# Order of the recurrence's scale levels and the projection matmuls between them

## The chip, the cores and the metric
The kernel runs on one core of a Trainium2 chip. The time is that of the device, in microseconds, of one execution of the whole program; a kernel's time is the median of its runs. Before the change it is 2439.49 us (three runs, 2434.9 to 2441.67).

## What is computed
An encoder trunk of one layer is applied to two requests, x_sample (1024 tokens) and x_prompt (512 tokens), with shared weights. The part that matters here is the recurrence of the mixer, for each of four heads and in both directions:

```python
q = silu(hq);  v = hi
f_f = lb[0] + (1 - lb[0]) * sigmoid(hff);  f_b = lb[1] + (1 - lb[1]) * sigmoid(hfb)
# per chunk, forward direction; the backward one is the same on flipped inputs
S_new = exp(b_last)[..., None] * S + einsum('bhsk,bhsv->bhkv', kc * exp(b_last - b), vc)
A = einsum('bhtk,bhsk,bhtsk->bhts', qc, kc, dec)        # dec: products of gates between s and t
o = einsum('bhts,bhsv->bhtv', A, vc) + einsum('bhtk,bhkv->bhtv', qc * exp(b), S)
hgo = rms_norm(o_f + o_b) * silu(hg)
```

Before it stands one input projection (h @ w_in), from which hq, hff, hfb, hi and hg come; around it stand an attention, an output projection and an expert layer with 16 experts.

## The kernel before
`build` runs, for the sample group and then the prompt group, `normalise`, `hgrn`, `attention` and `project_out`; then the experts and a last norm. The recurrence is `hgrn` (L543).

Tiling. Tokens lie along the free dimension, in blocks of 512 (`BLK`), `NB` = 2 blocks for the sample group and 1 for the prompt group. A block has four chunks of 128 (`BC`). Score banks `X[0..3]` are PSUM banks, one for each chunk of a block.

Levels. Instead of the three-index product of the reference, the scores of a chunk are made at eight scale levels. At level k TensorE multiplies the keys and queries as they stand, in small tiles on the diagonal (L688 for k < 6, 32x32 tiles; L694 for k = 6; L699 for k = 7), for the forward direction (d = 0, tiles q_f and k_f) and the backward one (d = 1, q_b and k_b). VectorE then multiplies gates into q and k for the next level (L819 for k = 0, L826, L827 and L829 for others), and this may begin when the level's products have been made (`level_read`); TensorE's next level waits for it (`updated`). After level 7 the step `diag` has VectorE multiply each score bank by masks (L870) and sum it up (L875); the next block's level 0 overwrites the banks and so waits for L870 (`masked`). Then keys are transposed (`k_rows`, L710, copied by ScalarE L796), states are made (`state`, L719, and VectorE L888 and L891), then the output (`o`, L739), its norm (`squares`, `mean`, `norm`: L804, L899, L952, L904) and its transpose (`mix`, L747, L912).

The projection for the next head is done beside it, by `Projection` (L410 and on). There are five columns (V, Q, FF, FB, G), each in two halves: ten units. A unit is the product of four 128x128 weight tiles with each block of tokens, as three matmuls each (high and low parts: L472, L473, L474), so 12 matmuls for each block. Its weights are split into `w_hi` (ScalarE, L453, waits until the unit before the last has been summed) and `w_lo` (VectorE, L457, waits for `w_hi`); TensorE's first matmul of a unit waits for `w_lo`. `w_hi` and `w_lo` have two slots; `w_raw`, loaded by SyncE (L447), has five, and a load waits for the split that frees its slot. When a column's two units are done it is landed by ScalarE (L767), the columns Q and G by VectorE too (L844).

Order. Each engine works through one list of steps, in order. `slots` is the list of recurrence steps; `beside` (L490) puts pieces of the projection between them: `piece(n)` is half a unit for one block (`CUTS` = 2: two weight tiles, 6 matmuls), and ahead of a unit's first piece it puts the step ("split", u + 1) for ScalarE and VectorE, behind a column's last piece ("land", column). `run_heads` runs three lists: the projection alone, a loop over three heads with both, and the last head's recurrence alone. Before the change the pieces are shared out evenly, one for each step (squares and mean not counted), with NB more at the start. Attention uses another function, `beside_at`, whose pieces are whole units for one block.

Of the kernel before, what the change touches and what calls it, by code (L numbers as in the profile page):

```python
# [15 lines left out]
P = 128  # L16
D = 1024
DT = D // P
BLK = 512
BC = BLK // P  # L20
# [4 lines left out]

COL_AQ, COL_AK, COL_AV, COL_HQ, COL_HFF, COL_HFB, COL_HI, COL_HG = range(0, 8 * BLK, BLK)
HALF = DT // 2
CUTS = 2
EXPERTS = 16
FF = 1024  # L30
FT = FF // P
# [455 lines left out]
        return steps  # L487


def beside(slots, proj, lead=0):  # L490


    pieces = CUTS * proj.units * proj.NB
    out, done, passed = [("split", 0)], 0, 0
    counted = lambda step: step[0] not in ("squares", "mean")
    total = sum(map(counted, slots))
    for step in slots:
        out.append(step)
        passed += counted(step)
        upto = lead + (pieces - lead) * passed // total  # L500
        for n in range(done, upto):
            out += proj.piece(n)
        done = upto
    return out


# [36 lines left out]
def hgrn(nc, g, T, w_in, masks_in, consts, banks, mem, chosen):  # L543
# [5 lines left out]
    NT, NB = T // P, T // BLK  # L549
    ident, slope_cols, lb, one_minus_lb, neg_lam, att_g, hg_g, carried, minus_half = consts  # L550
    with ExitStack() as c:
        sem = c.enter_context(semaphores(nc, f"h{g}"))
        X, FAR, TURN = banks[0:4], banks[4], banks[5]
        V, Q, FF_, FB, G = range(5)
        proj = Projection(sem, T, [COL_HI, COL_HQ, COL_HFF, COL_HFB, COL_HG], 5, [Q, G], banks[6:8], w_in, mem)
# [3 lines left out]
        level_read = [Signal(sem(f"level_{d}"), 8 * NB) for d in "fb"]  # L559
# [5 lines left out]
        v_rows = Signal(sem("v_rows"), NB)  # L565
        far_placed = Signal(sem("far_placed"), NB)
# [3 lines left out]
        gates = Signal(sem("gates"), 2)  # L570
        updated = [Signal(sem(f"updated_{d}"), 8 * NB) for d in "fb"]
# [14 lines left out]
        ds_bank = lambda d, b: (2 * d + b + 1) % 4  # L586
        slots = [("start",)] + [("v_rows", b) for b in range(NB)]
        for b in range(NB):
            slots += [("level", b, k) for k in range(8)] + [("diag", b)]
        for d in range(2):  # L590
            slots += [("k_rows", d, b) for b in range(NB)]
            slots += [("state", d, b) for b in (range(NB) if d == 0 else reversed(range(NB)))]
# [4 lines left out]
        first = beside([("none",)], proj)  # L597
        if g == 1:
            first = with_choices(first, "split", range(CHOICES_BEFORE["attention"][0]))
        stages = first, beside(slots, proj, NB), slots  # L600
        in_order = [s for s in slots if s[0] == "state"]
        nth = lambda step: in_order.index(step)
        first_state = lambda b, n, d: (b * BC + n == 0) if d == 0 else (b * BC + n == NT - 1)
# [1 line left out]
        x_uses = []  # L605
        for s in range(4):
            uses = []
            for step in slots:
                if step[0] == "level" and step[2] == 0:
                    uses.append((step, masked, BC * step[1] + s))  # L610
                if step[0] == "k_rows" and kt_bank(*step[1:]) == s:
                    uses.append((step, k_rows, NB * step[1] + step[2]))
                if step[0] == "state" and ds_bank(*step[1:]) == s:
                    d, b = step[1:]
                    done = min((b + 1) * BC, NT - 1) if d == 0 else min((NB - b) * BC, NT - 1)
                    uses.append((step, state[d], done - 1))
            x_uses.append(Uses(uses))
        far_uses = Uses([(("level", b, 6), far_placed, b) for b in range(NB)]
                        + [(("o", b), normed, b) for b in range(NB)])
        if NB == 2:  # L620
            far_uses = Uses([(("level", b, 6), far_placed, b) for b in range(NB)] + [(("o", 0), normed, 0)])
            x_uses[0].uses.append((("o", 1), normed, 1))
        o_bank = lambda b: FAR if b == 0 else X[0]
        o_uses = lambda b: far_uses if b == 0 else x_uses[0]
# [16 lines left out]
        with nc.Block() as block:  # L641
# [14 lines left out]
            def _(pe):  # L656
                start_signals(pe, [proj.summed, v_turned, *level_read, k_turned, added, o_summed, o_turned])

                def body(step, i, j):
# [3 lines left out]
                    elif kind == "v_rows":  # L663
                        b = step[1]
                        pe.wait_ge(proj.land_act.sem, proj.land_act.at(i, NB * V + b))
                        pe.wait_ge(*turn_uses.before(i, step))
                        for n in range(BC):
                            at = b * BLK + n * P
                            mm = pe.transpose(TURN[:, n * P:(n + 1) * P], mem.land[V][:, at:at + P], ident[:])
                        mm.then_inc(v_turned.sem, 1)  # L670
                    elif kind == "level":
                        b, k = step[1:]
                        if k == 6:
                            pe.wait_ge(*far_uses.before(i, step))
                        for d in range(2):
                            if k == 0:
                                pe.wait_ge(q_taken.sem, q_taken.at(i, d))
                                pe.wait_ge(k_made.sem, k_made.at(i, d))
                            else:
                                pe.wait_ge(updated[d].sem, updated[d].at(i, 8 * b + k - 1))  # L680
                            q, kk = mem.q[d], mem.k[d]
                            for n in range(BC):
                                at = b * BLK + n * P
                                if k == 0 and d == 0:
                                    pe.wait_ge(*x_uses[n].before(i, step))
                                if k < 6:
                                    for z in range(0, P, 32):
                                        mm = pe.matmul(X[n][z:z + 32, (6 * d + k) * 32:(6 * d + k + 1) * 32],  # L688
                                                       kk[:, at + z:at + z + 32], q[:, at + z:at + z + 32],
                                                       start=True, stop=True, tile_position=(0, z))  # L690
                                elif k == 6:
                                    for z in range(0, P, 64):
                                        s, t = z + 32 * d, z + 32 * (1 - d)
                                        mm = pe.matmul(FAR[s:s + 32, n * 96:n * 96 + 32], kk[:, at + s:at + s + 32],  # L694
                                                       q[:, at + t:at + t + 32], start=True, stop=True,
                                                       tile_position=(0, s))
                                else:
                                    s, t = 64 * d, 64 * (1 - d)
                                    mm = pe.matmul(FAR[s:s + 64, n * 96 + 32:n * 96 + 96], kk[:, at + s:at + s + 64],  # L699
                                                   q[:, at + t:at + t + 64], start=True, stop=True,  # L700
                                                   tile_position=(0, s))
                            mm.then_inc(level_read[d].sem, 1)
                    elif kind == "k_rows":
                        d, b = step[1:]
                        bank, uses = X[kt_bank(d, b)], x_uses[kt_bank(d, b)]
# [2 lines left out]
                        for n in range(BC):  # L708
                            at = b * BLK + n * P
                            mm = pe.transpose(bank[:, n * P:(n + 1) * P], mem.k[d][:, at:at + P], ident[:])  # L710
                        mm.then_inc(k_turned.sem, 1)
                    elif kind == "state":
                        d, b = step[1:]
# [8 lines left out]
                    elif kind == "o":  # L722
                        b = step[1]
# [7 lines left out]
                        for n in range(BC):  # L731
# [79 lines left out]
            def _(dve):  # L811
# [3 lines left out]
                def level(d, b, k, i):  # L815

                    if k == 0:
                        q = mem.q[d][:, b * BLK:(b + 1) * BLK]
                        dve.tensor_tensor(q, q, products(d, b, 0), ALU.mult).then_inc(updated[d].sem, 1)  # L819
                        return  # L820
                    half = 1 << (k - 1)
                    n = BLK // (2 * half)
                    q, kk = halves(mem.q[d], b, half), halves(mem.k[d], b, half)
                    f = products(d, b, k - 1).rearrange("p (n a) -> p n a", a=2)
                    late, early = (1, 0) if d == 0 else (0, 1)
                    dve.tensor_tensor(products(d, b, k), f[:, :, 0], f[:, :, 1], ALU.mult)  # L826
                    dve.tensor_tensor(q[:, :, late, :], q[:, :, late, :],  # L827
                                      f[:, :, early:early + 1].to_broadcast([P, n, half]), ALU.mult)
                    dve.tensor_tensor(kk[:, :, early, :], kk[:, :, early, :],  # L829
                                      f[:, :, late:late + 1].to_broadcast([P, n, half]),  # L830
                                      ALU.mult).then_inc(updated[d].sem, 1)

                def body(step, i, j):
# [19 lines left out]
                                              lb[:, bass.ds(i + d * HEADS, 1)], ALU.mult,  # L853
                                              ALU.add).then_inc(gates.sem, 1)
                    elif kind == "level":
                        b, k = step[1:]
                        for d in range(2):

                            dve.wait_ge(level_read[d].sem, level_read[d].at(i, 8 * b + k))
                            if k == 0:  # L860
                                dve.wait_ge(gates.sem, gates.at(i, d))
                            else:
                                dve.wait_ge(updated[d].sem, updated[d].at(i, 8 * b + k - 1))
                            level(d, b, k, i)
                    elif kind == "diag":
                        b = step[1]
                        for n in range(BC):
# [1102 lines left out]
```

## Time and profile before

| | us |
|---|---|
| median of the runs | 2439.49 (2434.9 to 2441.67) |
| span of the profiled execution, first to last instruction | 2427.6 |
| TensorE matmul busy | 2095.0 (86% of the span) |
| weight loads busy | 1801.6 (74%) |
| VectorE busy | 1484.0 (61%) |
| ScalarE busy | 1116.1 (46%) |
| GpSimd busy | 228.3 (9%) |
| mean granted clock of TensorE | 0.930 of full speed |
| loop of `hgrn`, sample group: starts of its passes and its end | 108.1, 197.5, 288.8, 378.8 |
| the same, prompt group | 986.9, 1032.4, 1077.8, 1124.3 |

The profiled execution's own time outside the span isn't given by the profile; the median of the runs lies 11.9 us above the span. The starts of passes are those of ScalarE's copy of the queries (L773).

How to read it. A timeline row has the start (us), the duration (us) of the group, the engine (PE is TensorE's matmul, PEld its weight load, DVE VectorE, ACT ScalarE, POOL GpSimd), the line, the operation, the tiles out<-in, their sizes, the count, and in brackets the idle time of the engine before it with what ended it. A window row has the stretch, its length, then the busy time of PE, PEld, DVE, ACT and POOL (with counts), the granted clock of TensorE as a part of full speed, the DMA share and GB/s. Matmuls overlap one another: their pace is the distance of two starts, not their duration. A level's products appear as two records each.

### The profile page before, as it was taken

Reading aid. Unit: us, or ns where it says so; the run is one execution under the profiler, and the core shown is the slowest. Engines: PE = TensorE matmul, PEld = TensorE weight load, DVE = VectorE, ACT = ScalarE, POOL = GpSimd, SP = SyncE. Lnnn points to the kernel's source line nnn. Section 1 sums busy time; section 2 is a strip of 40 time slices with the busy share of each in tenths; the row PEclk is TensorE's granted clock in tenths of the full one; section 3 lists DMA queues with packets and bytes.
Section 4 is the critical chain, followed back from the end, with each engine's and each line's share of the span. In section 5 each row is a group of like instructions: output and inputs, shape, how many; then the busy total and the mean of one; then the engine's idle time right before and its main releaser. Section 6 shows DMA issues by size and latency. Waiting matters only on the chain. (4 is left out here: it accounts for less than half of the span.)

```text
span 2427.6 us, 44323 instructions
## 1 busy us (share of the span) xinstructions
PE 2095.0 (86%) x16110; PEld 1801.6 (74%) x16110; DVE 1484.0 (61%) x2662; ACT 1116.1 (46%) x1941; POOL 228.3 (9%) x364
## 2 busy tenths in 40 slices
PE   4999997799897795998785849999999999999990
PEld 3777775577775684776574749999999999999990
DVE  3275577256666333667567756676666676666662
ACT  3222221256565323232464236666666666666652
POOL 1001101000000000111000001111111111111101
PEclk9999996899999896998897869999999999999995
DMA  3111100100000433220212257787777777777756
GB/s 116 45 30 33 32 11 2 56 22 19 22 4 1 151 119 107 67 57 9 77 43 85 98 184 225 241 250 235 252 241 242 241 245 237 238 243 244 237 169 229
DMA packets 178341, 313.16 MB, mean 129 GB/s; under 512 B 11825, under 2 KB 78001, under 8 KB 178225
## 3 DMA queue, kind: packets, MB, share of 16 engines
q1 hardware_dynamic: 169328, 280.08, 34.8%
q0 software_dynamic: 7168, 25.17, 5.2%
q10 hardware_dynamic: 1728, 6.29, 0.6%
q8 instruction: 82, 1.34, 0.2%
q14 instruction: 35, 0.28, 0.0%
HBM read 280.04 MB, written 31.46 MB: 128 GB/s over the span
## 5 line engine op out<-in xcount | busy, mean ns | idle before, releaser
L1802 DVE TENSOR_TENSOR we_lo<-raw,we_hi 128x1024 fp32r<-128x1024 f32 x384 | 466.0, 1223 | 219.4 <-ACT we_hi L1750 219.4
L1716 PE MATMUL psum<-x_parts,we_hi 128*128 128x384 f32 x2048 | 585.4, 360 | 2.9 <-DVE we_lo L1802 2.9
L1718 PE MATMUL psum<-x_parts,we_lo 128*128 128x192 f32 x2048 | 513.5, 251 | 0.0
L1750 ACT CAST we_hi<-raw 128x1024 fp32r<-128x1024 f32 x384 | 399.3, 1052 | 185.3 <-PE psum L1718 100.7
L1718 PEld LDWEIGHTS psum<-x_parts,we_lo 128*128 128x128 f32 x2048 | 392.3, 192 | 0.6
L1716 PEld LDWEIGHTS psum<-x_parts,we_hi 128*128 128x128 f32 x2048 | 385.5, 188 | 3.6 <-issue 3.0
L472 PE MATMUL psum<-hT_hi,w_hi 128*128 128x512 f32 x768 | 325.7, 424 | 62.1 <-DVE w_lo L457 62.0
L473 PE MATMUL psum<-hT_lo,w_hi 128*128 128x512 f32 x768 | 308.1, 401 | 0.0
L474 PE MATMUL psum<-hT_hi,w_lo 128*128 128x512 f32 x768 | 308.1, 401 | 0.0
L472 PEld LDWEIGHTS psum<-hT_hi,w_hi 128*128 128x128 f32 x768 | 149.2, 194 | 101.4 <-DVE w_lo L457 44.8
L474 PEld LDWEIGHTS psum<-hT_hi,w_lo 128*128 128x128 f32 x768 | 149.1, 194 | 33.7
L473 PEld LDWEIGHTS psum<-hT_lo,w_hi 128*128 128x128 f32 x768 | 149.9, 195 | 26.6
L457 DVE TENSOR_TENSOR w_lo<-h_w_raw,w_hi 128x512 fp32r<-128x512 f32 x80 | 57.3, 716 | 90.8 <-ACT w_hi L453 90.8
L767 ACT ACTIVATE h_land<-psum 128x512 f32<-128x512 f32 x60 | 35.9, 598 | 157.5 <-PE psum L474 157.4
L453 ACT CAST w_hi<-h_w_raw 128x512 fp32r<-128x512 f32 x80 | 49.3, 617 | 127.4 <-PE psum L474 115.5
L1732 PE MATMUL psum<-we_hi,hid_parts 128*128 128x512 f32 x256 | 103.0, 402 | 0.0
L1736 PE MATMUL psum<-we_lo,hid_parts 128*128 128x512 f32 x256 | 100.9, 394 | 0.0
L1735 PE MATMUL psum<-we_hi,hid_parts 128*128 128x512 f32 x256 | 100.8, 394 | 0.0
L1734 PE MATMUL psum<-we_hi,hid_parts 128*128 128x512 f32 x256 | 100.8, 394 | 0.0
L1733 PE MATMUL psum<-we_lo,hid_parts 128*128 128x512 f32 x256 | 100.6, 393 | 0.0
L121 POOL TENSOR_TENSOR carried_pool<-minus_half 128x1 f32<-128x1 f32 x48 | 13.7, 285 | 844.9 <-ACT result_s L1790 692.0
L1112 PEld LDWEIGHTS psum<-v_rows,k_rows 128*128 128x128 f32 x640 | 80.1, 197 | 16.9 <-ACT k_rows L1170 14.4
(245 smaller groups left out, 3598.4 us busy)
## 6 DMA issues: line engine op xcount, KB each, us to landing
raw<-in_w_gate SPq DMA_DIRECT2D x128, 512.0 KB, 4.6
raw<-in_w_up SPq DMA_DIRECT2D x128, 512.0 KB, 6.2
raw<-in_w_down SPq DMA_DIRECT2D x128, 512.0 KB, 5.7
h_w_raw<-in_w_in SPq DMA_DIRECT2D x80, 256.0 KB, 2.8
a_w_raw<-in_w_in SPq DMA_DIRECT2D x48, 256.0 KB, 2.8
o_land<-in_w_out SPq DMA_DIRECT2D x16, 512.0 KB, 5.2
y<-y_rows SPq DMA_DIRECT2D x12, 512.0 KB, 6.4
h_land<-in_x_s SPq DMA_DIRECT2D x8, 512.0 KB, 4.2
```

The source lines that it names most:

```text
L472: pe.matmul(out[:], mem.w_hi[:, u % 2, n, :], hi, start=(k == 0), stop=False)
L473: pe.matmul(out[:], mem.w_hi[:, u % 2, n, :], lo, start=False, stop=False)
L474: mm = pe.matmul(out[:], mem.w_lo[:, u % 2, n, :], hi, start=False, stop=(k == DT - 1))
L1716: pe.matmul(out[:, 0:2 * SLOTS], w_hi[:, s, at], x_parts[:, k, :, :], start=(k == 0), stop=False, skip_group_check=True)
L1718: mm = pe.matmul(out[:, SLOTS:2 * SLOTS], w_lo[:, s, at], x_hi[:, k, :], start=False, stop=(k == DT - 1), skip_group_check=True)
L1732: pe.matmul(out[2 + h][:], a, u, start=first, stop=False)
L1733: pe.matmul(out[2 + h][:], a, v, start=False, stop=False)
L1734: pe.matmul(out[2 + h][:], b, u, start=False, stop=last)
L1735: pe.matmul(out[h][:], both, u, start=first, stop=False)
L1736: mm = pe.matmul(out[h][:], both, v, start=False, stop=last)
L1750: act.copy(w_hi[:, n % PARTS, :], raw[:, s, :]).then_inc(hi.sem, 1)
L1802: dve.tensor_tensor(w_lo[:, n % PARTS, :], raw[:, n % RAW, :], w_hi[:, n % PARTS, :].bitcast(F32), ALU.subtract).then_inc(lo.sem, 1)
```

## The change
`CUTS` becomes 4: a piece is one weight tile for one block, 3 matmuls. The step ("level", b, k), which did both directions, becomes two steps ("level", b, k, d), on TensorE and VectorE. `beside` takes fixed numbers of pieces behind steps of some kinds: 2 behind `start`, 2 behind each `v_rows`, 1 behind each level of a direction, 6 behind each `diag`; the rest is shared evenly over the other steps. Waits belong to the same operations as before.

```diff
-CUTS = 2
+CUTS = 4
...
-def beside(slots, proj, lead=0):
+def beside(slots, proj, fixed=None):
...
+    fixed = {"squares": 0, "mean": 0} | (fixed or {})
     pieces = CUTS * proj.units * proj.NB
-    out, done, passed = [("split", 0)], 0, 0
-    counted = lambda step: step[0] not in ("squares", "mean")
-    total = sum(map(counted, slots))
+    rest = pieces - sum(fixed.get(step[0], 0) for step in slots)
+    others = sum(step[0] not in fixed for step in slots)
+    out, done, shared, passed = [("split", 0)], 0, 0, 0
     for step in slots:
         out.append(step)
-        passed += counted(step)
-        upto = lead + (pieces - lead) * passed // total
-        for n in range(done, upto):
+        if step[0] in fixed:
+            now = fixed[step[0]]
+        else:
+            passed += 1
+            now = rest * passed // others - shared
+            shared += now
+        for n in range(done, done + now):
             out += proj.piece(n)
-        done = upto
+        done += now
     return out
...
-            slots += [("level", b, k) for k in range(8)] + [("diag", b)]
+            slots += [("level", b, k, d) for k in range(8) for d in range(2)] + [("diag", b)]
...
-        stages = first, beside(slots, proj, NB), slots
+        stages = first, beside(slots, proj, {"start": 2, "v_rows": 2, "level": 1, "diag": 6}), slots
...
                     elif kind == "level":
-                        b, k = step[1:]
-                        if k == 6:
+                        b, k, d = step[1:]
+                        if k == 6 and d == 0:
                             pe.wait_ge(*far_uses.before(i, step))
-                        for d in range(2):
...
                     elif kind == "level":
-                        b, k = step[1:]
-                        for d in range(2):
-
-                            dve.wait_ge(level_read[d].sem, level_read[d].at(i, 8 * b + k))
...
+                        b, k, d = step[1:]
+                        dve.wait_ge(level_read[d].sem, level_read[d].at(i, 8 * b + k))
```

The lists of the prompt group's loop from level 5 to the first key transposes, written out (mmN is N matmuls; the sample group's are of the same kind, with 24 matmuls to a unit):

```
before  [level 5] split5 mm6 [level 6] mm6 [level 7] split6 mm6 [diag] mm6 land-FF [k_rows f] split7 mm6
after   [level 5 f] mm3 [level 5 b] mm3 land-Q [level 6 f] split5 mm3 [level 6 b] mm3 [level 7 f] mm3
        [level 7 b] mm3 [diag] split6 mm12 land-FF split7 mm6 [k_rows f] mm6
```

In the sample group, block 0: before, `[level 7] split4 mm6 [diag] mm12 [level 0 of block 1]`; after, `[level 7 b] mm3 [diag] mm6 split4 mm12 [level 0 f of block 1]`. The pieces between a pass's start and its first level go from 30 matmuls to 18 (sample) and from 18 to 12 (prompt).

## Rows read from the trace of the kernel before

**Rows 1.** The page: its first line, with the span.
```profile
span 2427.6 us, 44323 instructions
```

**Rows 2.** Windows: eight levels of the sample group's first pass.
```profile
118.80:135.60 16.80, 16.80 (x475) 12.70 (x474) 12.98 (x42) 2.32 (x4) 0.00 (x0) 1.00 0.12 35
```

**Rows 3.** Timeline of TensorE: a piece of six, a level, and the next piece.
```profile
119.61 0.50 PE L472 MATMUL psum<-hT_hi,w_hi 128*128 128x512 f32 x1
...
121.20 0.35 PEld L688 LDWEIGHTS psum<-q_f,k_f 128*32 128x32 f32 x32 [0.36 <-issue]
121.20 0.46 PE L688 MATMUL psum<-q_f,k_f 128*32 128x32 f32 x32
...
121.48 0.49 PE L688 MATMUL psum<-q_b,k_b 128*32 128x32 f32 x32
...
121.90 0.50 PE L472 MATMUL psum<-hT_hi,w_hi 128*128 128x512 f32 x1
...
122.23 0.39 PE L473 MATMUL psum<-hT_lo,w_hi 128*128 128x512 f32 x1
122.24 0.19 PEld L474 LDWEIGHTS psum<-hT_hi,w_lo 128*128 128x128 f32 x1
...
122.46 0.39 PE L474 MATMUL psum<-hT_hi,w_lo 128*128 128x512 f32 x1
```

**Rows 4.** Timeline and windows: the second pass, behind the mask sum of block 0.
```profile
232.81 0.79 PE L472 MATMUL psum<-hT_hi,w_hi 128*128 128x512 f32 x1
...
236.55 0.49 PE L472 MATMUL psum<-hT_hi,w_hi 128*128 128x512 f32 x1
...
229.40:240.00 10.60, 8.36 (x209) 5.87 (x209) 9.03 (x19) 1.11 (x2) 2.35 (x8) 0.84 0.08 22
```

**Rows 5.** Timeline of TensorE: first level products and key transposes of passes; 142.27 between.
```profile
118.77 0.32 PE L688 MATMUL psum<-q_f,k_f 128*32 128x32 f32 x14
...
142.27 0.27 PE L688 MATMUL psum<-q_f,k_f 128*32 128x32 f32 x8 [1.03 <-DVE h_masked L870]
...
162.68 0.38 PE L710 MATMUL psum<-ident,k_f 128*128 128x128 f32 x2
...
208.09 0.30 PE L688 MATMUL psum<-q_f,k_f 128*32 128x32 f32 x12
...
253.94 0.27 PE L710 MATMUL psum<-ident,k_f 128*128 128x128 f32 x1
...
299.36 0.24 PE L688 MATMUL psum<-q_f,k_f 128*32 128x32 f32 x4
...
344.48 0.38 PE L710 MATMUL psum<-ident,k_f 128*128 128x128 f32 x2
...
992.77 0.32 PE L688 MATMUL psum<-q_f,k_f 128*32 128x32 f32 x14
...
1013.09 0.38 PE L710 MATMUL psum<-ident,k_f 128*128 128x128 f32 x2
```

**Rows 6.** Timeline: the prompt group's level 7 and mask sum, on TensorE and VectorE.
```profile
1009.33 0.27 PE L699 MATMUL psum<-q_f,k_f 128*64 128x64 f32 x1
...
1010.04 0.16 DVE L826 TENSOR_TENSOR h_fend_f<-h_fup_f 128x4 f32<-128x4 f32 x1 [0.63 <-PE psum L699]
...
1010.79 0.16 DVE L826 TENSOR_TENSOR h_fend_b<-h_fup_b 128x4 f32<-128x4 f32 x1
...
1012.14 0.55 DVE L870 TENSOR_TENSOR h_masked<-psum,h_masks 128x384 f32<-128x384 f32 x1
...
1017.64 0.68 DVE L457 TENSOR_TENSOR w_lo<-h_w_raw,w_hi 128x512 fp32r<-128x512 f32 x1
...
1018.37 0.50 PE L472 MATMUL psum<-hT_hi,w_hi 128*128 128x512 f32 x1 [0.58 <-DVE w_lo L457]
```

**Rows 7.** Windows: the starts of two passes.
```profile
105.00:113.50 8.50, 6.41 (x22) 4.84 (x21) 4.94 (x6) 3.60 (x6) 3.58 (x6) 0.80 0.11 32
1029.00:1036.00 7.00, 4.91 (x22) 3.71 (x21) 3.26 (x6) 2.66 (x5) 2.18 (x4) 1.00 0.13 37
```

More of the change, by code:

```diff
@@ L608, in hgrn @@
             for step in slots:
-                if step[0] == "level" and step[2] == 0:
+                if step[0] == "level" and step[2:] == (0, 0):
                     uses.append((step, masked, BC * step[1] + s))
@@ L617, in hgrn @@
             x_uses.append(Uses(uses))
-        far_uses = Uses([(("level", b, 6), far_placed, b) for b in range(NB)]
+        far_uses = Uses([(("level", b, 6, 0), far_placed, b) for b in range(NB)]
                         + [(("o", b), normed, b) for b in range(NB)])
         if NB == 2:
-            far_uses = Uses([(("level", b, 6), far_placed, b) for b in range(NB)] + [(("o", 0), normed, 0)])
+            far_uses = Uses([(("level", b, 6, 0), far_placed, b) for b in range(NB)] + [(("o", 0), normed, 0)])
             x_uses[0].uses.append((("o", 1), normed, 1))
@@ L671, in body @@
                     elif kind == "level":
-                        b, k = step[1:]
-                        if k == 6:
+                        b, k, d = step[1:]
+                        if k == 6 and d == 0:
                             pe.wait_ge(*far_uses.before(i, step))
-                        for d in range(2):
-                            if k == 0:
-                                pe.wait_ge(q_taken.sem, q_taken.at(i, d))
-                                pe.wait_ge(k_made.sem, k_made.at(i, d))
-                            else:
[L680 to L702, printed above, removed]
@@ new lines, in body @@
+                        if k == 0:
+                            pe.wait_ge(q_taken.sem, q_taken.at(i, d))
+                            pe.wait_ge(k_made.sem, k_made.at(i, d))
+                        else:
+                            pe.wait_ge(updated[d].sem, updated[d].at(i, 8 * b + k - 1))
+                        q, kk = mem.q[d], mem.k[d]
+                        for n in range(BC):
+                            at = b * BLK + n * P
+                            if k == 0 and d == 0:
+                                pe.wait_ge(*x_uses[n].before(i, step))
+                            if k < 6:
+                                for z in range(0, P, 32):
+                                    mm = pe.matmul(X[n][z:z + 32, (6 * d + k) * 32:(6 * d + k + 1) * 32],
+                                                   kk[:, at + z:at + z + 32], q[:, at + z:at + z + 32],
+                                                   start=True, stop=True, tile_position=(0, z))
+                            elif k == 6:
+                                for z in range(0, P, 64):
+                                    s, t = z + 32 * d, z + 32 * (1 - d)
+                                    mm = pe.matmul(FAR[s:s + 32, n * 96:n * 96 + 32], kk[:, at + s:at + s + 32],
+                                                   q[:, at + t:at + t + 32], start=True, stop=True,
+                                                   tile_position=(0, s))
+                            else:
+                                s, t = 64 * d, 64 * (1 - d)
+                                mm = pe.matmul(FAR[s:s + 64, n * 96 + 32:n * 96 + 96], kk[:, at + s:at + s + 64],
+                                               q[:, at + t:at + t + 64], start=True, stop=True,
+                                               tile_position=(0, s))
@@ L703, in body @@
+                        mm.then_inc(level_read[d].sem, 1)
                     elif kind == "k_rows":
@@ L855, in body @@
                     elif kind == "level":
-                        b, k = step[1:]
-                        for d in range(2):
-                            dve.wait_ge(level_read[d].sem, level_read[d].at(i, 8 * b + k))
[L860 to L864, printed above, removed]
+                        b, k, d = step[1:]
+                        dve.wait_ge(level_read[d].sem, level_read[d].at(i, 8 * b + k))
+                        if k == 0:
+                            dve.wait_ge(gates.sem, gates.at(i, d))
+                        else:
+                            dve.wait_ge(updated[d].sem, updated[d].at(i, 8 * b + k - 1))
+                        level(d, b, k, i)
                     elif kind == "diag":
```

## The prediction, made before the changed kernel was timed
> **What bounds the kernel now.** I read the page first: the span is 2427.6 us [rows 1], and the diff touches only the loop over heads of `hgrn`. So I looked up where that loop lies: three passes for the sample group (1024 tokens, 108 to 379 us) and three for the prompt group (512 tokens, 987 to 1124 us), some 408 us together. The pass after each loop ("alone") has the same order before and after, the pass ahead of it has no levels, and attention takes its matmuls through another function, in the same order whether cut in two or four. Everything else of the span stays.
>
> Within a pass I read the table of windows. Over eight levels of the sample group TensorE is busy for all 16.80 us and VectorE for 12.98 of them [rows 2]. The few places of a pass where TensorE does wait are counted below. Elsewhere TensorE's own work sets the pace, and a level's products are not what anything waits for. The reader should then ask two things of the change: does it add work to TensorE, and does it take away or make waits of TensorE.
>
> **What a change of shape costs (the price of a cut).** In [rows 3] the six-matmul piece begins at 119.61 and the level's first product at 121.20, 1.59 us later. The steady pitch of these matmuls is 0.23 (122.23 to 122.46), six are 1.38. The other 0.21 are the two edges: 0.33 instead of 0.23 behind the first matmul (121.90 to 122.23), and as much ahead of the level. The forward direction then takes 0.28 (121.20 to 121.48), and the backward one, with the piece's first matmul behind it, 0.42 (121.48 to 121.90). One level is 0.70 + 1.59 = 2.29 us.
> In the changed order each direction stands alone: 0.42, and a piece of three: 3 x 0.23 + 0.21 = 0.90. Two of each are 2.64. A level costs 0.35 more. Levels inside the loop: 16 in each of three sample passes, 8 in each of three prompt passes, 72 together: 72 x 0.35 = +25.2 us. The trace of before has no direction alone between pieces. From below, the piece's two edges alone are 0.21, 15 us in all; from above, the idle time of 0.36 of the weight load ahead of a level [rows 3] and the 0.14, 36 us in all. I take 0.35, since each of its parts is a gap between starts in the same rows. A gain I exclude: no matmul goes away, and nothing in [rows 2] is left for it to fill.
>
> In [rows 3] the weight load of a level (128x32) waits 0.36 with the ending named as issue, while the load of a wide matmul starts at 122.24, with the matmul of 122.23 still under way. The Trainium skill, page "TensorE: Matmul & The Clock Gate", section "Architectural detail: the array is 16× 32×32, not 1× 128×128", says that TensorE's queue is a partial reorder window which can pull weight loads ahead of matmuls in flight. By that rule the cut would cost nothing, which is rival B. The wide loads agree with it, the level's loads do not.
>
> **Waits of the sample passes.** From a pass's first level product to its first key transpose the trace has 162.68 - 118.77 = 43.91, 253.94 - 208.09 = 45.85 and 344.48 - 299.36 = 45.12 us [rows 5]. Without a wait I get 16 levels x 0.70 (an estimate for the last two levels, which have other shapes) + 14 pieces x 1.59 + the 18 matmuls around the first mask sum, 4.35 + the last 12, 2.87 = 40.7. So the waits are 3.2 + 5.1 + 4.4 = 12.8 us. The largest stands at the mask sum of block 0: TensorE's next level needs the four score banks, and gets them as VectorE masks them, the last at 142.27 [rows 5]. Twice the clock falls behind it: the level from 232.81 to 236.55 takes 3.74 instead of 2.29, with a granted clock of 0.84 in the stretch around it [rows 4], so half speed (1.2 GHz) for part of it.
> Now 21 matmuls stand between the last product of level 7 and the next level, where 18 stood, and the weight split that VectorE did ahead of the masks now stands behind them. Counted from the start of that last product: TensorE is through after 0.5 + 0.1 + 21 x 0.23 + 0.1 = 5.5 us. VectorE starts the level's update after 0.71, takes 0.75, and its fourth mask ends 3 x 1.38 + 0.55 later, at 6.15 [rows 6] (the same operations in the prompt group). About 0.6 of the wait stays, and 0.2 where the query tile lands between two levels. I take 0.8 a pass: 12.8 - 2.4 = -10.4 us. Bounds: 0 and -12.8. Block 1's mask sum has no such wait before or after: key transposes follow it, and the split of unit 6 is ahead of it.
>
> **The split behind the prompt group's mask sum.** Here a unit has only 12 matmuls. At the mask sum the new list has: mask sum, split 6, the four pieces of unit 5, land, split 7, two pieces of unit 6, key transposes. VectorE works its list in order, so `w_lo` of unit 6 is made only when the whole mask sum is done; TensorE's first matmul of unit 6 waits for it, and the transposes, states and output of the head are queued behind that matmul. Before, split 6 stood ahead of the mask sum. Counted from the start of the last product of level 7: VectorE 0.71 (1009.33 to 1010.04) + 0.75 (to 1010.79) + mask sum 5.50 (1012.14 to 1017.64) + split 0.68 + 0.05 = 7.7 [rows 6]. TensorE 0.5 + the level's three matmuls and twelve of unit 5, 3.5 = 4.0. It stands still for 3.7 us, in three passes: +11.1. Bounds: 3.0 to 4.5 each, as VectorE is level with TensorE or late from level 6.
> A wait like that lets the clock fall: at the starts of passes, where TensorE waits about 2.2 us for the first split, it fell in four of six ([rows 7] has one of each kind, 0.80 and 1.00). One fall costs 3.74 - 2.29 = 1.45 us [rows 4]; 3 x 1.45 = +4.4, bound below by nothing.
> What goes in the prompt passes: of 1013.09 - 992.77 = 20.32 us [rows 5] 19.6 is work by the same count, 0.7 waits, and TensorE's 0.58 for the split at 1018.37 [rows 6], which was late behind the mask sum and now follows at once on split 6. Together 1.3 x 3 = -3.9.
>
> **Edits with no price.** At the start of a pass 12 fewer matmuls (6 in the prompt group) stand ahead of level 0; they come back later in the same in-order list, so TensorE's total is the same. Keys and gates are ready by then (GpSimd's and ScalarE's parts begin when the pass begins). The last piece of a pass is 9 or 6 matmuls instead of 12 behind the last transpose: VectorE's mix is over before the landing either way. ScalarE's splits move with VectorE's, and wait for nothing new. SyncE's load of a weight slot waits for the split that frees it; a slot is used again five units later, 60 matmuls of 0.23 us in the prompt group, so that split 6 comes some 4 us later is hidden; should it not be, ScalarE's next splits would be late by as much.
>
> **The sum.** 25.2 - 10.4 + 11.1 + 4.4 - 3.9 = +26.4 us. On the profiled span of 2427.6 that is 2454.0. Around the span lie 11.9 us up to the median of 2439.49; I count them as unchanged: 2465.9 us. The likeliest case's own spread is about 2456 to 2476. A measurement of this kernel can tell about 0.3%, 7 us, from no change.
>
> **Rivals.**
> A. The late split is absorbed: VectorE reaches the prompt group's mask sum earlier than I count, and nothing of the 15.5 us for wait and clock comes. 2450.4 us, still slower. Against it: VectorE cannot start the mask sum before the last update, and 5.5 us stand against 3.5. Chance 0.07.
> B. Cuts are free: level loads are pulled ahead when only three matmuls stand before them. Without the 25.2 us: 2440.7, no difference. Against it, the 0.33 us starts in [rows 3] came with operands ready. Chance 0.07.
> C. VectorE's chain (levels, masks, states, norm) sets a pass's length, and TensorE's matmuls only fill. Then the cuts fit in, and what counts is that level 0 starts 12 (6) matmuls earlier: 3 x (2.8 + 1.4) = 12.6 us, 2426.9, faster. It decides as soon as TensorE has over 0.35 us idle in a level; [rows 2] shows none. Chance 0.04.
> D. The clock falls within the levels too, as wide matmuls are a smaller part of each (1.38 of 2.64 instead of 2.29). With two falls a pass, 12 x 1.45 = 17.4 more: 2483.3. For it, falls at [rows 4]; against it, those came behind a wait. Chance 0.06.
> My sum has 0.76.
> The range 2449 to 2478 takes in my case and A. Slower by over 0.3%: 0.76 + 0.07 + 0.06 less a little for a sum that comes out small, 0.87; within 0.3%: 0.08; faster: 0.05.
>
> **What would show it.** In the windows, a sample pass longer by about 2 us and a prompt pass by about 7. In TensorE's timeline, a level of 2.6 us with its two directions apart and 0.33 at four edges; if the edges were at 0.23 the first term is wrong. At the prompt group's mask sum, the first matmul of unit 6 released by `w_lo`, 3.7 us late, and a granted clock of half behind it. At the sample group's block 0, the wait for the masks down from 2.1 to about 0.6 us. The prediction is wrong if the levels' pace is not TensorE's, or if the late split waits for something else.

## The result

| | median us (runs) | ratio to before, 95% interval |
|---|---|---|
| before | 2439.53 (4; 2434.9 to 2441.67) | |
| changed | 2463.33 (4; 2459.17 to 2464.37) | 1.0101 (1.0085 to 1.0117) |

The change costs 23.8 us, 1%; the forecast was +26.4, to 2465.9. Page of the changed kernel, its first line and its busy times, with their share of the span and the number of instructions; [rows 1] is the first line of before:

```profile
span 2457.0 us, 44323 instructions
PE 2119.0 (86%) x16110; PEld 1802.5 (73%) x16110; DVE 1488.4 (61%) x2662; ACT 1117.4 (45%) x1941; POOL 229.8 (9%) x364
```

No instruction was added, and TensorE's matmul busy time grew from 2095.0 to 2119.0. The profiled execution took 2459.17, 2.2 us more than its span. If the same lies around the span of before (2427.6), that profiled execution took about 2430, 10 us less than its kernel's median. So the two profiles differ by 29.4 us and the medians by 23.8. I therefore compare kernels in two ways: by their medians, and by the length of the passes in the profile. Windows over the three sample passes, then over the three prompt passes, first of before, then of the changed kernel (stretch, length, busy times of PE, PEld, DVE, ACT, POOL, granted clock, DMA):

```profile
108.14:378.77 270.63, 257.61 (x3640) 204.42 (x3640) 167.17 (x420) 66.96 (x169) 32.73 (x72) 0.97 0.09 26
986.95:1124.26 137.31, 127.78 (x1816) 100.06 (x1816) 90.58 (x225) 41.34 (x102) 19.31 (x45) 0.99 0.17 48
```
```profile
106.53:382.54 276.01, 267.61 (x3640) 200.76 (x3640) 170.26 (x420) 67.50 (x169) 34.93 (x72) 0.99 0.09 26
991.18:1152.88 161.70, 144.52 (x1816) 106.84 (x1816) 91.66 (x225) 42.19 (x103) 19.34 (x45) 0.92 0.14 41
```

The reader sees 5.4 us more in the sample group and 24.4 more in the prompt group, together 29.8; outside the passes nothing moved by more than 1.6 us. VectorE's own time in the passes grew by 4.2 us. The granted clock went up a little in the sample passes and down to 0.92 in the prompt passes. Since the low level is half of full speed, a mean of 0.92 means that a steadily busy TensorE falls behind by 8% of the time: 161.7 x 0.08 = 13 us, against 137.3 x 0.01 = 1.4 before.

The levels, in TensorE's timeline of the changed kernel; [rows 3] has the same place before:

```profile
114.15 0.46 PE L692 MATMUL psum<-q_b,k_b 128*32 128x32 f32 x32
114.54 0.50 PE L472 MATMUL psum<-hT_hi,w_hi 128*128 128x512 f32 x1
114.88 0.39 PE L473 MATMUL psum<-hT_lo,w_hi 128*128 128x512 f32 x1
...
115.43 0.46 PE L692 MATMUL psum<-q_f,k_f 128*32 128x32 f32 x32
115.82 0.50 PE L472 MATMUL psum<-hT_hi,w_hi 128*128 128x512 f32 x1
...
116.72 0.46 PE L692 MATMUL psum<-q_b,k_b 128*32 128x32 f32 x32
```

A direction with its piece of three takes 1.28 us (114.15 to 115.43), the two of a level 2.57 (114.15 to 116.72), where a level of before took 2.29. The edges are as they were, 0.34 behind the first wide matmul (114.54 to 114.88) and 0.32 ahead of the next level (115.11, the start of the last wide matmul, to 115.43). Six levels of the first prompt pass show the same over a longer stretch; the row of 1006.63 is of before, whose level 0 starts at 992.77 [rows 5], the other two are of the changed kernel:

```profile
1006.63 0.35 PE L694 MATMUL psum<-q_f,k_f 128*32 128x32 f32 x10
```
```profile
995.65 0.45 PE L692 MATMUL psum<-q_f,k_f 128*32 128x32 f32 x30
...
1011.06 0.44 PE L698 MATMUL psum<-q_f,k_f 128*32 128x32 f32 x15
```

From level 0 to level 6 before took 13.86 us, 2.31 a level, and the changed kernel 15.41, 2.57 a level. The single level of [rows 3], 2.29, was a little short of the mean.

The prompt group's late split, on both engines ([rows 6] has the place before):

```profile
1015.11 0.68 PE L703 MATMUL psum<-q_b,k_b 128*64 128x64 f32 x8
...
1016.57 0.55 DVE L872 TENSOR_TENSOR h_masked<-psum,h_masks 128x384 f32<-128x384 f32 x1
...
1021.29 0.80 DVE L877 TENSOR_REDUCE h_diag<-h_masked 128x32 f32<-128x384 f32 x1
1022.00 1.28 DVE L457 TENSOR_TENSOR w_lo<-h_w_raw,w_hi 128x512 fp32r<-128x512 f32 x2
...
1022.82 0.79 PE L472 MATMUL psum<-hT_hi,w_hi 128*128 128x512 f32 x1 [3.40 <-DVE w_lo L457]
1023.40 0.63 PE L473 MATMUL psum<-hT_lo,w_hi 128*128 128x512 f32 x1
```

The mask sum ends, the splits of units 6 and 7 follow, and TensorE starts unit 6 after 3.40 us without work. Then its second matmul comes 0.58 behind the first, where at full clock it is 0.33. The window behind the wait:

```profile
1022.20:1029.00 6.80, 6.18 (x17) 4.93 (x18) 1.08 (x2) 0.59 (x1) 2.36 (x8) 0.50 0.27 77
```

The clock is at its lower level, 1.2 GHz, for 6.8 us, twice as long as I had counted.

What TensorE's matmuls waited for, in the list of waits over the sample passes (total us, times, longest), first before, then the changed kernel:

```profile
PE psum L472 <- DVE w_lo L457: 6.3, 3, 2.1
PE psum L688 <- DVE h_masked L870: 5.1, 6, 1.0
PE psum L688 <- issue: 1.9, 3, 0.8
PE psum L688 <- DVE k_b L829: 0.5, 1, 0.5
```
```profile
PE psum L472 <- DVE w_lo L457: 6.3, 3, 2.1
PE psum L472 <- DVE h_land L848: 1.8, 3, 0.6
PE psum L692 <- DVE h_masked L872: 0.8, 3, 0.3
```

The wait for the masks did fall from 5.1 to 0.8 us, the others of the levels from 2.4 to nothing, and one of 0.6 in each pass is new. With two small rows not shown (0.5 us, L743) the sum is 9.4 us, against 13.8 before. The first row is the wait at the start of a pass; it is 6.3 us in every kernel below too.

### The profile page after: what moved, and what is told of

It is laid out like the page before. It is cut to its first block and busy times, and to the rows that moved or that the text cites. A ratio compares the mean times of both kernels' runs of the same rounds, so it can differ in the third digit from the quotient of the medians.

```text
span 2457.0 us, 44323 instructions
## 1 busy us (share of the span) xinstructions
PE 2119.0 (86%) x16110; PEld 1802.5 (73%) x16110; DVE 1488.4 (61%) x2662; ACT 1117.4 (45%) x1941; POOL 229.8 (9%) x364
## 5 line engine op out<-in xcount | busy, mean ns | idle before, releaser
L472 PE MATMUL psum<-hT_hi,w_hi 128*128 128x512 f32 x768 | 335.7, 437 | 72.7 <-DVE w_lo L457 70.8
L1381 PE MATMUL psum<-hT_hi,w_hi 128*128 128x512 f32 x192 | 78.8, 410 | 15.5 <-DVE hT_lo L1499 15.5
```

What stands on the lines that cost most here:

```text
L472: pe.matmul(out[:], mem.w_hi[:, u % 2, n, :], hi, start=(k == 0), stop=False)
```

## The experiments

In the tables "passes" are the sample and prompt passes of each profile, by length, with the granted clock over them.

### The split back ahead of the mask sum (e1)

```diff
-        stages = first, beside(slots, proj, {"start": 2, "v_rows": 2, "level": 1, "diag": 6}), slots
+        both = beside(slots, proj, {"start": 2, "v_rows": 2, "level": 1, "diag": 6})
+        if NB == 1:
+            at = both.index(("diag", 0))
+            both.remove(("split", 6))
+            both.insert(at, ("split", 6))
+        stages = first, both, slots
```

> The changed kernel with one step moved: in the prompt group's loop the split of unit 6 stands ahead of the mask sum again, on ScalarE and VectorE. My theory: the wait of TensorE for that split (3.4 us, three times) and the low clock behind it go, 15.5 us by the terms of the sum; the mask sum now begins behind the split, so the next split (unit 7) may come up to 0.9 us late in each pass: 2448 to 2451 us. Rival A (the late split is absorbed, the cuts are all of the loss): 2463, as the changed kernel.

Measured: 2445.93 us (12 runs), ratio 1.003 (1.0017 to 1.0043); 17.4 us less than the changed kernel. Its passes:

```profile
107.41:381.83 274.42, 266.05 (x3640) 199.58 (x3640) 170.17 (x420) 67.45 (x168) 34.86 (x72) 0.99 0.09 26
994.81:1138.31 143.50, 134.30 (x1816) 99.61 (x1816) 91.94 (x225) 41.86 (x102) 19.25 (x45) 0.99 0.16 46
```

The prompt passes account for it (161.70 to 143.50, 18.2 us; the sample passes differ by 1.6), and their clock is back at 0.99. One step of 0.7 us on VectorE, moved past a step of 5.5 (ScalarE's half of the split moves with it), is worth 0.7% of the kernel. The spans of the two profiles differ by 7.8 us only (2457.0 and 2449.2): the stretch outside the passes, which no edit here touches, took 2019.3 us in the one and 2031.3 in the other, and lies between 2019.3 and 2031.6 in the profiles whose passes are given here. So medians and passes are compared, not spans. The next split is late now, as the expectation had it:

```profile
1027.88 0.50 PE L472 MATMUL psum<-hT_hi,w_hi 128*128 128x512 f32 x1 [0.76 <-DVE w_lo L457]
```

Rival A is out. The expected 2448 to 2451 was 2 us too high at its lower end, since the clock gave back more than three times 1.45 us.

### The directions together again (e2)

```diff
-    rest = pieces - sum(fixed.get(step[0], 0) for step in slots)
+    count = lambda step: 2 * step[3] if step[0] == "level" else fixed[step[0]]
+    rest = pieces - sum(count(step) for step in slots if step[0] in fixed)
...
-            now = fixed[step[0]]
+            now = count(step)
```

> The changed kernel with the two directions of a level together again (no matmul piece behind the forward one, two pieces behind the backward one); the rest, with six pieces at each mask sum, as changed. My theory: 72 cuts at 0.35 us go, 2463.3 - 25.2 = 2438 us (2434 to 2443). Rival B (a cut is free): 2463.

Measured: 2442.53 us (12 runs), ratio 1.0019 (1.0007 to 1.0031); 20.8 less than the changed kernel. Rival B is out; the size is 4 us under the forecast. Passes, and the waits in the sample passes:

```profile
107.82:369.36 261.54, 250.51 (x3640) 198.69 (x3640) 168.05 (x420) 67.53 (x169) 36.65 (x72) 1.00 0.10 27
979.09:1130.32 151.23, 134.19 (x1816) 104.81 (x1816) 90.23 (x225) 42.17 (x102) 19.30 (x45) 0.94 0.15 44
...
PE psum L693 <- issue: 3.1, 4, 1.0
PE psum L693 <- DVE k_b L834: 1.2, 3, 0.4
PE psum L744 <- issue: 0.5, 3, 0.2
PE psum L693 <- DVE q_b L824: 0.5, 2, 0.2
```

No wait for the masks is left, and 4.8 us of others within the levels stand where before had 2.4. Most are named issue: TensorE pauses within the backward products of a level (3.1 us in four), and the profile shows nothing that it waits for. The three for `k_b` (0.41 us each) stand behind VectorE's landing of a column, two steps of 0.7 us between the updates of two levels. So the shift of matmuls alone took only 2.2 us of waits out of the sample passes (13.8 to 11.6, with the 6.3 at the starts). Yet these passes are 9.1 us shorter than before (270.63 to 261.54): the rest is the clock, 0.97 before and 1.00 here.

The late split is still there, and its wait is nearly as long as in the changed kernel. But the low clock behind it is half as long:

```profile
1008.52 0.49 PE L472 MATMUL psum<-hT_hi,w_hi 128*128 128x512 f32 x1 [3.24 <-DVE w_lo L457]
...
1009.80:1013.20 3.40, 3.40 (x12) 2.72 (x11) 0.00 (x0) 0.59 (x1) 0.74 (x4) 0.50 0.53 152
```

The other two prompt passes of e2 have the same: a wait of 3.21 us and 3.4 us at half clock.

### The cut alone (e3)

The order of before, with each level's six matmuls divided between its directions (a split that stood behind a level stands between its directions now):

```diff
...
+    for n, step in enumerate(slots):
+        out.append(step)
+        if step[0] == "level" and step[3] == 0:
+            for m in range(2 * done, 2 * done + 1):
+                out += proj.piece(m)
+            continue
...
+        first = 2 * done + (step[0] == "level")
+        for m in range(first, 2 * upto):
+            out += proj.piece(m)
+        done = upto
```

> The kernel before with the cut alone: each level in two directions with three of its six matmuls between them, every other piece and split where it was. My theory: 2439.5 + 25.2 = 2465 us (2459 to 2470), a little less if the cut lets VectorE reach the sample group's mask sum earlier. Rival B: 2440. Rival C (VectorE's chain sets a pass's length): under 2440.

Measured: 2449.69 us (8 runs), ratio 1.0042 (1.0026 to 1.0058): +10.3, not +25.2. This is a miss by 15 us, though of the forecast sign. Rivals B and C are out. Passes, and waits of the sample passes:

```profile
106.32:382.04 275.72, 265.89 (x3640) 198.72 (x3640) 170.22 (x420) 66.52 (x168) 32.51 (x72) 1.00 0.09 26
993.93:1136.06 142.13, 134.45 (x1816) 99.38 (x1816) 92.66 (x225) 41.30 (x103) 18.85 (x45) 0.99 0.16 47
...
PE psum L713 <- DVE h_masked L893: 4.0, 6, 1.0
```

Two things paid for the difference. The cut took away waits of its own: of 7.5 us within the levels of before 4.0 are left, with no piece more at the mask sum. And the clock stayed up for all of the sample passes (1.00 against 0.97, 270.6 x 0.03 = 8 us), even behind the mask wait, which was 0.3 + 1.0 us here and 0.67 + 1.03 before. That this is no accident of one profile, the runs say: each has its span and mean granted clock on record, and span x (1 - clock), the time lost to the clock, averages 176.2 us over the 8 runs of e3 and 186.3 over the 30 of before beside them, 10 less, unsure by 3. (It counts time at the low clock in which TensorE stood idle too.) Why the cut keeps the clock up isn't shown.

### Both repairs (e4), and once more (e7)

The edits of e1 and e2 in one kernel.

> Both repairs: directions together, and the prompt group's split of unit 6 ahead of the mask sum; what is left of the change is the shift of matmuls from the start of a pass to the mask sums. My theory: the shift alone is worth the waits it removes, 10.4 and 3.9 us, less up to 2.7 for the later mask sum: 2425 to 2430 us, faster than before. Rival: the removed waits come back elsewhere in the pass, 2439.

> The kernel of e4 once more, beside e6 on the same chip: 2431.7 us, within 0.1%.

Measured: 2431.65 (11 runs), ratio 0.9966 (0.9953 to 0.9978); the second time 2429.15 (12 runs), 0.9966 (0.995 to 0.9982). Faster than before, but by 0.34%, 8 us, where 10 to 14 were expected. Passes of e4, then of e7:

```profile
106.95:372.44 265.49, 255.35 (x3640) 202.36 (x3640) 167.80 (x420) 67.42 (x168) 35.87 (x72) 0.98 0.10 27
981.89:1119.53 137.64, 128.12 (x1816) 100.31 (x1816) 90.52 (x225) 41.87 (x103) 19.27 (x45) 0.99 0.17 48
```
```profile
106.66:369.60 262.94, 252.36 (x3640) 200.14 (x3640) 168.04 (x420) 67.44 (x169) 36.41 (x72) 0.99 0.10 27
981.13:1118.79 137.66, 128.10 (x1816) 100.37 (x1816) 90.59 (x225) 41.88 (x103) 19.28 (x45) 0.99 0.17 48
```

The prompt passes gained nothing over before (137.31), the sample passes 5 to 8 us. The rival, that waits come back elsewhere, holds for the prompt group. In the sample group it nearly does: what was gained there is mostly clock. Over all runs the time lost to the clock, span x (1 - clock), averages 178.4 us for e4 and 186.3 for before beside it, 176.2 for e7 and 184.1 for before beside that: 7.9 less both times, unsure by about 2. What is left, span x clock, is the same (2250.8 and 2250.7; 2251.6 and 2251.6). So as far as these averages tell, the shift of matmuls made the kernel faster by the clock and not by work or waits saved.

### What the edge of a piece is made of (e5)

```diff
...
-                                for z in range(0, P, 32):
-                                    mm = pe.matmul(X[n][z:z + 32, (6 * d + k) * 32:(6 * d + k + 1) * 32],
-                                                   kk[:, at + z:at + z + 32], q[:, at + z:at + z + 32],
-                                                   start=True, stop=True, tile_position=(0, z))
+                                mm = pe.matmul(X[n][:, (6 * d + k) * 32:(6 * d + k + 1) * 32],
+                                               kk[:, at:at + P], q[:, at:at + 32], start=True, stop=True)
```

> The changed kernel with the products of levels 0 to 5 in another shape: one full-width product for each chunk (128x128 keys loaded, 32 query columns) in place of four loads of 32 columns at tile positions. The scores it makes are not the reference's, since keys of one quarter meet queries of another; the waits are the same. It tells what the edges of a piece are made of. If they belong to the narrow loads at a tile position: the starts at the edges (0.33 us ahead of a level and behind the first wide matmul) go to about 0.23 ahead of the level, as they are at the value transposes, which wait for semaphores too. If they belong to the wait for a semaphore: 0.33 as before. The direction's own time falls or stays, four loads of 128 columns against sixteen of 32; the whole 2450 to 2465 us.

Measured: 2521.25 us (4 runs), ratio 1.0339 (1.0306 to 1.0372): 58 us more than the changed kernel, outside the range expected. The reading it was made for is clear. Timeline, loads included:

```profile
114.74 0.40 PE L474 MATMUL psum<-hT_hi,w_lo 128*128 128x512 f32 x1
114.74 1.09 PEld L691 LDWEIGHTS psum<-q_f,k_f 128*128 128x128 f32 x8
114.97 0.97 PE L691 MATMUL psum<-q_f,k_f 128*128 128x32 f32 x8
115.78 0.47 PE L472 MATMUL psum<-hT_hi,w_hi 128*128 128x512 f32 x1
...
116.09 0.39 PE L473 MATMUL psum<-hT_lo,w_hi 128*128 128x512 f32 x1
```

The level's first load begins with the last wide matmul, at 114.74, and its product 0.23 behind it: the edge of 0.33 ahead of a level is gone, with the same waits for semaphores. So that edge belongs to the narrow load at a tile position, which is not pulled ahead (0.36 idle before it in [rows 3]), and not to the semaphores. The edit changed three things at once, the width, the tile position, and with them TensorE's switch between two shapes of load; which of them makes the edge isn't shown. The other edge, behind the first wide matmul, stays: 0.31 (115.78 to 116.09). Four full loads for a direction take 0.81 us (114.97 to 115.78), sixteen narrow ones 0.39; the narrow form is the right one, edges and all. By the Trainium skill, "TensorE: Matmul & The Clock Gate", section "The mechanism", a load overlaps matmuls in flight only where its row group differs. Here full-height loads overlap a full-height matmul, and the narrow ones, full-height too, do not: in these rows it isn't the row group that decides. The same section of the Trainium skill also lets a load be pulled ahead when it targets the background weight buffer, which would cover the full loads; no run here shows which buffer a load goes to.

### One more repair (e6), and the two best halves (e8)

VectorE's mask sum becomes four steps. In the prompt group's loop the split of unit 7 stands ahead of the last:

```diff
...
+            late = ("split", 7) in steps and ("diag", 1) not in steps
+            out += [("mask", step[1], n) for n in range(BC - late)]
+            held = ("mask", step[1], BC - 1) if late else None
+        out.append(step)
+        if held and step == ("split", 7):
+            out.append(held)
```

e6 also puts eight pieces (`"diag": 4 + 2 * NB`) at the sample group's mask sums; e8 leaves them at six.

> The kernel of e4 with two more repairs: in the prompt group VectorE does three of the four masks, then the split of unit 7, then the fourth, so that no split is late; in the sample group eight instead of six pieces (24 matmuls) stand at a mask sum. My theory: the 0.8 us wait of each prompt pass and the 0.5 to 0.7 us at each sample mask sum go, about 4 us less than e4. Rival (other waits take their place): as e4.

> The kernel of e6 with six pieces at the sample group's mask sums again, as in e4; only the prompt group keeps the repair of e6. From the passes of e6 and e7: sample 262.9 (e7) and prompt 133.0 (e6) us, some 4 us under e4: 2425 us, ratio to before 0.995. Rival: e6's sample passes were longer by chance of the clock and not by the eight pieces, then as e6, 2427.

Measured: e6 2427.25 (12 runs), 0.9964 (0.9949 to 0.9979); e8 2429.08 (8 runs), 0.9971 (0.996 to 0.9983). Passes of e6, then of e8:

```profile
107.82:374.22 266.40, 253.10 (x3640) 200.82 (x3640) 168.22 (x420) 67.12 (x169) 33.67 (x72) 0.99 0.10 27
983.64:1116.69 133.05, 125.78 (x1816) 98.99 (x1816) 91.06 (x225) 41.88 (x103) 18.20 (x45) 1.00 0.18 50
...
PE psum L711 <- issue: 4.1, 5, 1.3
PE psum L762 <- DVE state_b L911: 2.1, 3, 0.7
PE psum L472 <- ACT h_land L790: 1.7, 3, 0.6
```
```profile
106.61:368.31 261.70, 251.96 (x3640) 199.91 (x3640) 167.80 (x420) 67.51 (x168) 36.51 (x72) 0.99 0.10 27
977.51:1110.30 132.79, 125.44 (x1816) 98.85 (x1816) 90.99 (x225) 41.90 (x102) 18.23 (x45) 1.00 0.17 50
```

The prompt passes are 4.3 and 4.5 us shorter than before. Eight pieces do not help the sample group: of the three rows of waits in e6's sample passes the wait for the landing is new, the one for the state was 0.2 us in e8, and those within the levels 3.5 in all, since the pieces were taken from there. By passes e8 is the shortest, 394.5 us against 407.9 of before; by the runs e4, e6, e7 and e8 cannot be told apart (all near 0.9967). All four beat both kernels. The expected 2425 for e8 was 4 us too low.

### The changed kernel once more (e9)

> The changed kernel once more, for a second profile of its own. If the low clock behind the prompt group's late split belongs to that wait, each of the three passes has it again, for 3.4 or 6.8 us; if it came by chance, some have none.

One run, 2463.86 us. The window behind the wait, in this second profile:

```profile
1022.00:1028.70 6.70, 5.73 (x16) 4.56 (x17) 1.44 (x3) 0.58 (x1) 2.35 (x8) 0.50 0.27 78
```

The clock is at half in the same place as in the first, for 6.8 us, and so in the other two passes. The low clock belongs to the wait; its length doesn't follow from the wait's alone, as e2 has 3.4 us behind 3.24.

## Why the prediction was right, point by point

The time, the sign and the mechanism held: cuts and the late split cost what they cost where the prediction had put them. But that the total came within 3 us is in part luck. The price of the cuts was 7 us too large, the clock behind the late split 6 too small, and these errors nearly cancel. To see the terms without the clock, I take from each kernel's passes the length times (1 - granted clock), with the clock from the windows (two digits, so about 1.4 us unsure for the sample passes and 0.7 for the prompt passes):

| | passes | lost to the clock | rest |
|---|---|---|---|
| before | 407.9 | 9.5 | 398.4 |
| changed | 437.7 | 15.7 | 422.0 |
| e1, split ahead | 417.9 | 4.2 | 413.7 |
| e2, joined | 412.8 | 9.1 | 403.7 |
| e3, cut alone | 417.9 | 1.4 | 416.4 |
| e4, joined and ahead | 403.1 | 6.7 | 396.4 |

**The price of a cut.** Expected 25.2 us for 72. Changed less e2, e1 less e4, and e3 less before, the cut in three surroundings, are 18.3, 17.3 and 18.0 us in the last column: 0.25 us a cut. The profiles are one execution each; over all runs, span x clock averages 2280.2 us for the changed kernel (4 runs), 2269.7 for e1, 2260.7 for e2, 2271.4 for e3, 2250.8 for e4 and 2250.7 for before (30), so the same pairs are 19.5, 18.9 and 20.7, each unsure by 2 to 3. A cut costs 0.24 to 0.29 us. By the medians the same three pairs are 20.8, 14.3 and 10.3, and look as if they disagreed; the clock makes most of the difference. The step that was mis-sized is "A level costs 0.35 more": the rows show 2.57 - 2.29 = 0.28, since a direction alone took 0.39 and not 0.42, and over six levels 2.57 - 2.31 = 0.26, 18.7 us for 72. The cut also saves small waits within the levels (e3); I had given all saved waits to the shift.

**Waits of the sample passes.** Expected -10.4. Of TensorE's waits 13.8 - 9.4 = 4.4 us went, and of the clock's loss 270.6 x 0.03 - 276.0 x 0.01 = 5.4. But with the cut undone (e2) the shift alone took 2.2 us of waits, so the step "12.8 - 2.4" failed as the account of the shift: it assumed that nothing but the mask sum's wait would change when level 0 comes earlier, and e2 has new pauses in the levels. What those named issue are stays open. That e2's sample passes are 9.1 us shorter even so is the clock: before, it fell five times in them, twice behind the masks and three times at the starts, which this term did not count; in e2 it never fell.

**The late split.** Expected 3.7 us of wait in each of three passes; 3.40 in the trace. VectorE's path from the last product of level 7 to TensorE's start of unit 6 was forecast at 7.7 us and took 7.7 (1015.11 for the product's start, 1022.82). The 0.3 us lie on TensorE's side, whose last matmul counts as busy to its end. With the split moved (e1) 17.4 us of the median went, against 15.5 forecast.

**The clock behind it.** Expected 1.45 a pass; the stretch at half speed was 6.8 us, not 3.4, so about 3.4 us lost a pass. This is the term that was too small: it makes up for what the first one was too large. In e2, behind nearly the same wait, it was 3.4 us, as forecast, so a term that goes by the length of the wait could not have given both.

**The prompt group's saved waits.** Expected -3.9. In the changed kernel the wait of 0.58 is gone in each pass, and one of 0.3 for level 6 too, 2.6 us. Once the late split is repaired they come back: e4 has 137.64 us against 137.31, as the split of unit 7 became late in turn (0.78 us a pass). The whole gain came only with the masks in steps (e8, 132.79).

**Rival D.** The clock did not fall within the levels. In the changed kernel's sample passes it fell twice, at the starts of the second and third (199.5 and 291.7 us), and in e3, with the same 72 cuts, not at all.

**Edits with no price.** Outside the passes the profiles differ by 1.6 us at the first pass's start and by under 1 us behind it. SyncE's later load is not among the waits of either group.

**Anchoring.** I added the sum to the median and called 11.9 us the time around the span. That name was wrong: 2.2 us lie around a span, and for the rest the profiled execution was faster than the median. The sum on the median was still the right use of it.

What stays open: why the clock fell at some starts of passes and not at others. The same 2.1 us wait stands at each; before had three falls there in the sample passes, e2 and e3 none. The two profiles of the changed kernel have them in the same places, but those of e4 and e7, one kernel too, do not: three falls at the starts of the sample passes in the one, and one in the other. So the order alone does not decide it, a few us of a pass's length are a matter of the execution, and no run here tells by what.

## What to carry to other kernels

Where engines work through one fixed list, moving a filler moves what rides with it: here the weight split of the next unit slid behind a 5.5 us step of the engine that makes it, and that cost 17 us, about as much as all 72 cuts. List for each moved step who makes its operand and what stands ahead of that on the maker's own list. Cutting a block of wide matmuls around small ones has a price for each change of shape (about 0.26 us here), and is worth it only where it removes a longer wait. When two variants differ by under 1%, take the clock's share out of each before attributing the difference, over all runs where they have it and not from one profile.

## What the runs showed of the hardware that I had not expected

- The 0.10 us extra ahead of a group of products with 32-column loads goes with the narrow load at a tile position, not with its semaphore wait: with 128-column loads and the same waits the next start is at 0.23 (e5). The 0.10 behind the group's first wide matmul stays (0.31 in e5).
- A wait of TensorE of 3.40 us was followed by 6.8 us at half clock, at the same times in two profiles of one kernel (changed, e9); one of 3.24 us by 3.4 us (e2); waits of 2.1 us by 3.4 us or none, and not alike in two profiles of one kernel (e4, e7).
- The kernel before ran from 2426.4 to 2446.1 us over the 23 runs beside e6 and e7. A single profile can be 10 us off the median, nearly half of the effect studied here.
